# Three short VectorE steps of the samples' attention, placed at dot products 88, 92 and 96 instead of 74, 78 and 84

## The reference, cut to what matters

```
    s = jnp.einsum('bqhgd,bhqnld->bhgqnl', qf, k_sel)
    p_sel = masked_softmax(s - m[..., None] * dist, mask, axis=(-2, -1))
    o_sel = jnp.einsum('bhgqnl,bhqnld->bqhgd', p_sel, v_sel)
```

```
        act = jax.nn.gelu(jnp.einsum('nd,nhkd->nhk', hb.astype(f32), u_tab[eid].astype(f32)))
        out = jnp.einsum('nhk,nhkd->nd', gate * act, v_tab[eid].astype(f32))
```

## Time and profile before

| | before |
|---|---|
| median of 3 runs | 2667.0 us (2664.21 to 2672.71) |
| the profiled execution, whole | 2663.13 us |
| its span, first to last instruction | 2661.4 us |
| VectorE busy | 1094.2 us (41%) |
| GpSimd busy | 711.7 us (27%) |
| TensorE matmul busy | 1826.8 us (69%) |
| moved by DMA | 894.06 MB, mean 336 GB/s |
| tile 1's dot products, first to last | 1797.61 to 2199.97 us of the span |

### The profile page before, as it was taken

How to read it: one execution, slowest core, us unless ns; L and a number is a source line. 1 busy time by engine, 2 the same in 40 slices (tenths; PEclk the granted TensorE clock), 3 DMA queues, 4 the chain that set the end, 5 groups by cost and what they waited for, 6 DMA issues and landing times.

```text
span 2661.4 us, 31428 instructions
## 1 busy us (share of the span) xinstructions
PE 1826.8 (69%) x11621; PEld 1194.4 (45%) x11621; DVE 1094.2 (41%) x1939; ACT 418.5 (16%) x946; POOL 711.7 (27%) x600
## 2 busy tenths in 40 slices
PE   5799999998889943676639897664343206666673
PEld 2477777877868943566526564111111102201120
DVE  2200002416673597676660117228775780000014
ACT  0100000122272211533400101201001000000011
POOL 1000000000010036443462223335652543232233
PEclk8899999999999975787869999776656557676785
DMA  9889997435037689999999999999998999999997
GB/s 385 292 302 349 327 337 250 146 91 162 11 121 232 213 295 417 411 413 411 413 419 400 419 416 418 413 414 379 394 392 297 352 399 400 352 422 421 421 421 310
DMA packets 285366, 894.06 MB, mean 336 GB/s; under 512 B 26383, under 2 KB 160579, under 8 KB 212059
## 3 DMA queue, kind: packets, MB, share of 16 engines
q0 software_dynamic: 78384, 569.78, 52.8%
q1 hardware_dynamic: 178946, 296.39, 31.6%
q10 hardware_dynamic: 27884, 25.92, 3.0%
HBM read 883.35 MB, written 17.21 MB: 338 GB/s over the span
## 4 chain that ended last, share of the span: by engine, by line
DMA 37%; PE 34%; DVE 10%; SPq 7%; issue 4%; POOL 4%; ACTq 2%; ACT 1%; DVEq 0%; POOLq 0%; PEldq 0%
DMA sb_ring<-in_peer_v_dram,sb_modT 18%; PE ps L419 14%; DMA sb_ring<-in_peer_u_dram,sb_dist 14%; SPq L1404 5%; POOL sb_ring L2693 4%; DMA sb_ring<-in_w_ada_dram 3%; PE ps L2613 3%; DVE sb_ring L2160 3%; SPq L1403 3%; PE ps L213 3%; PE ps L1913 2%; DMA sb_pT<-in_cache_sel_kv_dram 1%; PE ps L2332 1%; PE ps L2369 1%; PE ps L1710 1%
## 5 line engine op out<-in xcount | busy, mean ns | idle before, releaser
L2160 DVE SCALAR_TENSOR_TENSOR sb_ring<-sb_ring,sb_pT 128x2048 f32<-128x2048 f32 x264 | 602.9, 2292 | 230.9 <-DMA sb_ring<-in_peer_u_dram,sb_dist 187.3
L2693 POOL DMA_INDIRECT sb_ring<-in_peer_u_dram,sb_dist x256 | 398.7, 1557 | 559.3 <-DVE sb_ring L2160 386.9
L2613 PE MATMUL ps<-sb_ring,sb_xT 128*32 128x512 f32 x2048 | 339.5, 757 | 196.9 <-DMA sb_ring<-in_peer_v_dram,sb_modT 194.1
L2693 POOL DMA_INDIRECT sb_ring<-in_peer_v_dram,sb_modT x256 | 253.7, 991 | 547.9 <-PE ps L2613 527.8
L419 PE MATMUL ps<-sb_hT,sb_ring 128*128 128x264 f32 x1664 | 374.8, 387 | 0.0
L419 PEld LDWEIGHTS ps<-sb_hT,sb_ring 128*128 128x128 f32 x1664 | 314.8, 190 | 66.0 <-issue 13.0
L2613 PEld LDWEIGHTS ps<-sb_ring,sb_xT 128*32 128x32 f32 x2048 | 50.2, 121 | 424.6 <-DMA sb_ring<-in_peer_v_dram,sb_modT 377.4
L2448 PE MATMUL ps<-sb_ident,sb_ring 128*128 128x128 f32 x512 | 105.3, 364 | 134.3 <-DMA sb_ring<-in_cache_cmp_kv_dram 109.2
L2448 PEld LDWEIGHTS ps<-sb_ident,sb_ring 128*128 128x128 f32 x512 | 79.3, 186 | 158.0 <-DMA sb_ring<-in_cache_cmp_kv_dram 127.4
L2502 ACT ACTIVATE sb_pT<-ps 128x256 f32<-128x256 f32 x256 | 127.7, 660 | 98.5 <-PE ps L2448 98.2
L1710 PE MATMUL ps<-sb_work,sb_pT 128*64 128x512 f32 (+1 forms) x96 | 68.0, 800 | 98.2 <-ACT sb_work L1588 96.3
(11 more groups left out here) (604 smaller groups left out, 2338.2 us busy)
## 6 DMA issues: line engine op xcount, KB each, us to landing
sb_ring<-in_w_ada_dram SPq DMA_DIRECT2D x48, 2048.0 KB, 10.9
sb_ring<-in_w_in_dram SPq DMA_DIRECT2D x26, 2048.0 KB, 14.3
sb_ring<-in_peer_wq_dram SPq DMA_DIRECT2D x18, 1024.0 KB, 15.3
sb_ring<-in_cache_cmp_kv_dram SPq DMA_DIRECT2D x68, 256.0 KB, 12.4
sb_ring<-in_w_out_dram SPq DMA_DIRECT2D x8, 2048.0 KB, 8.7
sb_ring<-in_cache_cmp_kv_dram ACTq DMA_DIRECT2D x60, 256.0 KB, 10.5
sb_ring<-in_w_out_dram SPq DMA_DIRECT2D x14, 1024.0 KB, 9.6
sb_pT<-in_peer_wq_dram SPq DMA_DIRECT2D x14, 1024.0 KB, 16.9
```

The source lines that it names most:

```text
L2160: dve.scalar_tensor_tensor(R3(rows), R3(rows), 1.0, h2r[t] if t < NT else R3(h2w), ALU.mult, ALU.mult, accum_out=(dots if t < NT else dots ...
L2613: mm = pe.matmul(bank(G % 2)[32 * q:32 * q + 32, :], w, rows[:, 512 * q:512 * q + 512], start=j == 0, stop=j == last)
L2693: pool.indirect_dma_start(rbuf[e % NBUF], None, io["peer_u" if kind == "u" else "peer_v"][0], bass.IndirectOffsetOnAxis(index, 0)).then_in ...
```

## The change

One table of numbers changes; no instruction is added or removed. What a step does, and on what it waits, stays as it was.

```
-        SAMP_DOTS = (26, 34, 74, 78, 84)
+        SAMP_DOTS = (26, 34, 88, 92, 96)
```

## The result

The changed kernel took 2648.1 us (median of 20 runs, 2641.38 to 2666.47), the kernel before 2665.54 us (20 runs, 2660.7 to 2678.69): ratio 0.9933, 95% interval 0.9922 to 0.9945, so 17.4 us less, 14.7 to 20.8 by the interval. The forecast was 2645.0 us, 22 us less. The profiled span went from 2661.4 to 2644.6 us, 16.8 us.

What follows compares the result with a forecast made beforehand. The prediction took the DMA engines, loading gathered rows, as the bound, starved around step 7's wait; 23.0 - 1.2 = 22 us off the profiled 2663.13 gave 2641, or 2645.0 us on the median's scale, range 2636 to 2656.

Steps and rivals of the forecast that it cites:

- Step 7's wait: VectorE's 24.06 us wait for TensorE's scores at the head of step 7 falls away whole, with 13 us to spare.
- does not change: TensorE and ScalarE work from the last key item to the scores' release stays 8.25 us.
- The second rival: Step 7's wait only moves, as gathers slow the last key item: 2659 to 2667 us; 7 in 100 with other no-gain reasons.
- 8 to 14: How many dot products back each of the three steps in VectorE's stream was said to move.
- The DMA engines' missing bytes: From 2018.55 to 2091.75 the engines moved 19.68 MB, 50.2 us' worth at 392 GB/s: 23.0 us less, 20 to 29 by rows.
- The first rival: Steps close together on VectorE hold up GpSimd's issue 11.60 us again, costing 10 us: 2655 us, 12 in 100.
- the rule of the Trainium skill: For GpSimd's gather issues: speaks against denser VectorE, but each issue waits for one instruction only, so the sum stays at 22.
- `samp_p` and the gelu: Step 9 and `samp_p` come 13.3 us later; ScalarE's margin before the gelu shrinks to 24 us and hides it.
- gives back some of their DMA time: Part of the last value items lands after the dot products: 0.5 MB, 1.2 us taken off the gain.
- the time from there to the end 461 us as before: From the last dot product to the kernel's end, the time was to stay at 461 us.

Runs made afterwards that it cites:

- Experiments 1: Against the kernel before, only steps 8 and 9 move, to dot products 92 and 96, step 7 stays at 74: 2661.18 us, ratio 0.9979.
- 3: Against the kernel before, step 7 at dot product 80, steps 8 and 9 at 92 and 96: 2656.21 us, ratio 0.9954.
- 4: Against the kernel before, step 7 at dot product 77, steps 8 and 9 at 92 and 96: 2658.16 us, ratio 0.9973.
- the repeat: The changed kernel (steps at 88, 92, 96) run once more with a second trace, against the kernel before: 2645.08 us, ratio 0.9926.
- experiments 2: The packed kernel: steps 7, 8 and 9 at dot products 88, 89 and 90, against the kernel before: 2645.72 us, ratio 0.9925.
- experiment 5: Against the kernel before, steps 7 and 8 at dot products 88 and 92, step 9 put off to 116: 2663.77 us, ratio 0.9993.
- 7: Against the kernel before, steps at 88, 92 and 100, and the wait for step 8's own last instruction removed: 2650.69 us, ratio 0.9942.
- experiment 8: Against the kernel before, steps 7, 8 and 9 spread to dot products 88, 94 and 102: 2648.59 us, ratio 0.9936.
- experiments 6: Against the kernel before, steps at 88, 89 and 90, plus a VectorE wait for step 9's own last instruction: 2644.17 us, ratio 0.9925.
- 10: The kernel before, its order kept (74, 78, 84), plus a VectorE wait for step 9's own last instruction: 2660.15 us, ratio 0.9987.

## Why the prediction was right, and where its size was off

**Step 7's wait.** Forecast: reached at 2060.4, scores at 2047.1, 13 us to spare. Trace: reached at 2060.24, scores at about 2050, 10 us to spare. The last key item kept its distance to the one before (2040.13 - 2014.96 = 25.2 us, 26.0 assumed); the start 2.2 us later in the span and some 1.5 us more for the work behind the item, which "does not change" by the forecast, make up the difference. 1.1 us of that lie in TensorE's second stretch of this work: its granted clock is 0.50 there (2042.87 to 2045.89), in the kernel before 0.88 (2037.52 to 2039.40). The wait fell away whole. Experiments 1, 3 and 4 bring it back in three lengths, and the gain goes with it. The second rival (a wait that only moves) is out. The steps moved by 14, 14 and 12 products, not by "8 to 14"; the sums use the right numbers.

**The DMA engines' missing bytes.** 23.0 us by bytes, 20 to 29 by rows; the stretch shrank by 21.3 us and by 22.1 in the repeat. That the price is the bytes and not the wait's 24.06 us agrees with experiments 3 and 4: the first microseconds of a wait are carried by gathers in flight.

**The first rival.** Its long issue is there in seven of the other orders at 11.3 to 11.6 us (experiments 1 to 5, 7 and 8), and in the changed kernel at 4.96. The forecast held because VectorE ran out of landed rows sooner behind step 9 in the changed kernel; and where the issue was long it cost at most 5 us of the stretch, half of the price given. There is luck in this: the 23.0 us count the 5.1 us lost around the long issue as won, and the prediction prices the issue's staying but gives no reason why it should go; experiments 5 and 8, with step 7 at the same place, show that it need not. That the issue hangs on how close the steps stand, as this rival had it, is wrong (experiment 8). In the prediction the rule of the Trainium skill (SBUF — State Buffer, section "SBUF: two separate sides") stood beside it: GpSimd's descriptors wait until the VectorE instruction that holds the shared port pair ends. The issues of 1.91 and 2.75 us agree with that. Those of 7.17 and 11.60 us don't, and experiments 6 and 7 show what they hang on in these two places: whether VectorE waits for its last small instruction before the dot products that follow. Why the wait lets GpSimd in at every later product boundary is not shown. In both places that instruction is a `tensor_scalar` of 64 x 64; behind the two instructions of 128 x 2048 and other kinds (lines 2240 and 2247) no wait is needed, and whether the kind or the size makes the difference wasn't tried.

**`samp_p` and the gelu.** 13.3 us later forecast, 12.9 measured; margin 24 us forecast, 27.22 measured. Experiment 5 takes the margin away and gets 2663.77 us, near the kernel before.

**The term that was mis-sized** is the last: "gives back some of their DMA time", 1.2 us, and with it "the time from there to the end 461 us as before". It measured 463.7 us in the changed kernel, 466.0 in the repeat and 468.5 with the added wait, 2.3 to 7.1 us more than the 461.4 of before. The three other kernels with step 9 at 84 or 90 (experiments 2, 6 and 10) have 462.0 to 462.9, the five with it at 96 to 102 and another place for step 7 or 8 (experiments 1, 3, 4, 7 and 8) 463.0 to 465.0. It isn't more bytes behind the products. The windows of the first 130 us of the `v` phase and the rest, in the kernel before and then in the changed one:

```profile
2199.97:2329.97 130.00, 82.97 (x625) 30.85 (x629) 0.39 (x3) 6.60 (x18) 37.40 (x40) 0.72 1.02 375
2329.97:2661.40 331.43, 193.25 (x1082) 37.88 (x1074) 47.89 (x88) 30.82 (x52) 106.22 (x100) 0.71 0.96 399
```

```profile
2180.89:2310.89 130.00, 79.21 (x604) 27.31 (x607) 0.37 (x3) 6.23 (x17) 36.61 (x39) 0.71 1.00 359
2310.89:2644.60 333.71, 194.26 (x1106) 39.52 (x1099) 47.90 (x88) 31.23 (x53) 106.35 (x100) 0.71 0.97 400
```

130.00 x 375 and 331.43 x 399 GB/s are 181.0 MB, 130.00 x 359 and 333.71 x 400 are 180.2 MB: no more is moved, but in the first 130 us it moves slower, 359 GB/s here, 351 and 349 in the two other traces of this order. The 0.5 MB that the forecast moved behind the products were 0.1: the queues of SyncE and ScalarE move 16.1 MB in the stretch of before and 15.9 in the changed one's. Part of the loss can be seen at TensorE, whose stream has the picked values' steps (line 1751) between the tokens. Its waits for those items in the first 145 us of the `v` phase, before and then changed (total, times, longest):

```profile
PE ps L1751 <- DMA sb_ring<-in_cache_sel_kv_dram: 13.5, 1, 13.5
PE ps L1751 <- DMA sb_pT<-in_cache_sel_kv_dram: 2.8, 2, 1.9
```

```profile
PE ps L1751 <- DMA sb_pT<-in_cache_sel_kv_dram: 16.7, 2, 10.3
PE ps L1751 <- DMA sb_ring<-in_cache_sel_kv_dram: 4.7, 2, 4.5
```

That is 16.3 us before, 21.4 in the changed kernel, and 23.0 and 27.6 in the two other traces of this order. While TensorE stands there no buffer comes free, and behind the longest of these waits in the changed kernel (2260.89 to 2270.89) the DMA engines are busy 0.60 of the time at 140 GB/s. The waits don't explain all: the packed kernel has 21.8 us of them and 462.0 us to the end. Nor can it be the lateness of the value items alone: with step 9 at 102 they come later still, and the rate is 370. Why these waits grew stays open. The other part of the missing 4.6 us of the median is not tied to a place: the stretch's start alone moves by 16 us between traces of a kernel that is the same up to there, and in the repeat the gain was 2664.65 - 2645.08 = 19.6 us.

**A better version.** The three nearest, packed with the added wait (2644.17 us), packed (2645.72) and the changed order with the added wait (2646.07), can't be told from the changed kernel, whose repeat took 2645.08: their ratios, 0.9925, 0.9925 and 0.9923, stand beside 0.9926.

## What to carry to other kernels

A step that waits inside a stream of ring consumers belongs behind the point where its producer is surely done; its worth is the bytes that the DMA engines did not move around it, and a ring in flight carries the first part of a wait for less than its length (here 9.31 us for 0.4 to 4.7 us of the stretch). Before moving it, follow what the step releases to the next engine that queues work behind it, and keep that margin: 20 dot products further cost the whole gain here. Where GpSimd's gather issues are long against a dense VectorE stream, a wait for the last small instruction ahead of it is a cheap thing to try; here it shortened the issue each time, and the time by no amount that the runs could tell, except in the order of before, where it is at the edge (0.9987, 0.9973 to 1.0).

## What the runs showed of the hardware that was not expected

A gather's issue on GpSimd, 0.94 us with VectorE idle and 1.91 to 2.75 us between dot products of 2.21 us, lasted 11.60 us, until VectorE paused, when the dot products followed a `tensor_scalar` of 64 x 64 that VectorE did not wait for; adding the wait brought it to 2.75 us and removing one elsewhere made 7.17 us. Behind a `tensor_tensor` and a `scalar_tensor_tensor` of 128 x 2048 without a wait it was 2.75 and 2.74 us. A ring of six 1 MB gathers, with 0.46 MB of other loads, kept the DMA engines at 412 GB/s through 9.31 us in which VectorE consumed nothing.
